# A second feed-forward input layer in seven half-width products instead of eight, with its weight sums split between GpSimd and VectorE

## The reference, cut to what matters

```
h  = x @ w_in                       # 1024 -> 2 x 2816 features
h  = conv_w[0]*h[t-1] + conv_w[1]*h[t] + conv_w[2]*h[t+1] + conv_b      # per feature, along the tokens
a, b = first 2816 features of h, last 2816 features of h
y  = (a * silu(b)) @ w_out          # 2816 -> 1024
```

## Time and profile before

| what | value |
|---|---|
| median of 3 runs | 1866.51 us (1865.86 to 1866.53) |
| time of the profiled execution | 1865.64 us, its span 1863.5 us |
| TensorE busy | 1715.4 us, 92% of the span |
| VectorE, ScalarE, GpSimd busy | 959.3, 377.4, 0.2 us |
| the changed stage, TensorE's first product to its last | 914.15 to 1066.17 us |
| granted TensorE clock there | 1.00 of full speed |

### The profile page before, as it was taken

How to read it: one execution, slowest core, us unless ns; L and a number is a source line. 1 busy time by engine, 2 the same in 40 slices (tenths; PEclk the granted TensorE clock), 3 DMA queues, 4 the chain that set the end, 5 groups by cost and what they waited for, 6 DMA issues and landing times.

```text
span 1863.5 us, 33795 instructions
## 1 busy us (share of the span) xinstructions
PE 1715.4 (92%) x14324; PEld 1358.6 (73%) x14324; DVE 959.3 (51%) x2032; ACT 377.4 (20%) x909; POOL 0.2 (0%) x4
## 2 busy tenths in 40 slices
PE   7999999999999999999999999999999767666676
PEld 4565687888888886776888898888887555545554
DVE  1488879666667328787544484577433111111112
ACT  0343413211110014222211102113402000000001
POOL 0000000000000000000000000000000000000000
PEclk9999999999999999999999999999999988888888
DMA  9524342222231214554343633331297999999997
GB/s 386 210 114 155 131 168 91 86 74 74 82 146 34 113 46 176 220 178 175 106 166 135 248 137 136 136 136 69 103 382 313 426 428 429 429 428 428 428 429 310
DMA packets 36164, 394.24 MB, mean 212 GB/s; under 512 B 3936, under 2 KB 7264, under 8 KB 14816
## 3 DMA queue, kind: packets, MB, share of 16 engines
q1 hardware_dynamic: 36064, 392.79, 52.3%
HBM read 391.72 MB, written 1.05 MB: 211 GB/s over the span
## 4 chain that ended last, share of the span: by engine, by line
PE 77%; DMA 19%; DVE 3%; issue 1%; ACT 0%; SPq 0%; DVEq 0%
PE bank L664 20%; DMA ring<-w_moe 19%; PE bank L1966 14%; PE bank L1680 11%; PE bank L2225 3%; PE bank L3788 3%; PE bank L2271 3%; PE bank L963 2%; PE bank L3554 2%; PE bank L2221 1%; PE bank L1268 1%; PE bank L718 1%; PE bank L872 1%; PE bank L2878 1%; PE bank L1253 1%; PE bank L2968 1%
## 5 line engine op out<-in xcount | busy, mean ns | idle before, releaser
L664 PE MATMUL bank<-layer_input,ring 128*128 128x256 f32 x1136 | 249.6, 380 | 0.0
L664 PEld LDWEIGHTS bank<-layer_input,ring 128*128 128x128 f32 x1136 | 214.4, 190 | 31.2 <-issue 2.7
L1680 PE MATMUL bank<-arena,ring 128*128 128x256 f32 (+1 forms) x940 | 167.4, 336 | 0.0
L1680 PEld LDWEIGHTS bank<-arena,ring 128*128 128x128 f32 x940 | 148.1, 191 | 14.6 <-issue 0.4
L3788 PE MATMUL bank<-arena 128*32 128x128 f32 x2008 | 77.8, 318 | 52.6 <-DMA arena<-w_moe 50.0
L3940 DVE TENSOR_TENSOR arena<-arena,bank 128x128 f32<-128x128 f32 x32 | 9.2, 288 | 218.1 <-PE bank L3788 218.1
L1966 PE MATMUL bank<-arena 128*128 128x256 f32 x504 | 115.7, 379 | 0.0
L3788 PEld LDWEIGHTS bank<-arena 128*32 128x32 f32 x2008 | 66.8, 128 | 64.4 <-DMA arena<-w_moe 60.1
L1966 PEld LDWEIGHTS bank<-arena 128*128 128x128 f32 x504 | 95.7, 190 | 13.2 <-DVE arena L2095 0.2
L3788 PE MATMUL bank<-ring,arena 128*32 128x128 f32 x1920 | 67.7, 301 | 27.6 <-DMA ring<-w_moe 27.3
L664 PE MATMUL bank<-arena 128*128 128x128 f32 (+2 forms) x400 | 86.6, 371 | 1.0 <-DVE arena L3768 1.0
(11 more groups left out here) (530 smaller groups left out, 2788.2 us busy)
## 6 DMA issues: line engine op xcount, KB each, us to landing
arena<-w_moe SPq DMA_DIRECT2D x45, 2048.0 KB, 25.8
ring<-w_moe SPq DMA_DIRECT2D x45, 2048.0 KB, 26.5
ring<-w_ffn_in SPq DMA_DIRECT2D x22, 2048.0 KB, 7.9
ring<-w_proj SPq DMA_DIRECT2D x7, 3072.0 KB, 10.3
ring<-w_ada_late SPq DMA_DIRECT2D x8, 2560.0 KB, 9.3
ring<-w_ffn_out SPq DMA_DIRECT2D x6, 2816.0 KB, 9.8
ring<-w_na_pair SPq DMA_DIRECT2D x5, 2048.0 KB, 7.9
arena<-w_far SPq DMA_DIRECT2D x16, 512.0 KB, 5.1
```

Source lines behind the costliest of these rows:

```text
L664: last = pe.matmul(out, a, b, start=(k == 0), stop=(k == len(lhs) - 1))
L1680: last = eng.matmul(out, w[:, k * P:(k + 1) * P], x[:, k, :], start=(start and k == 0), stop=(stop and k == half - 1), skip_group_check=True)
```

## The change

The second feed-forward input is rewritten. Weights and inputs are cut in two along k (features 0 to 511 and 512 to 1023) and in two along the tokens (128 and 128), and the value and gate rows give the other cut of the weights. Then for each f from 2 to 21 TensorE does seven products of 4 steps with 128 columns, in place of 16 steps with 256 columns. f = 0 and 1 (chunk 0) are done as before.

- Four sums of token blocks (128x512 each) are formed once, on VectorE.
- Four sums of weight blocks (128x1024) are needed for every pair of f. For pair 1 VectorE does all four. For pairs 2 to 10 GpSimd does the first and third and VectorE the second and fourth.
- ScalarE copies five running sums (128x128) per f out of PSUM, does the middle tap with the bias (from SBUF for f from 2 on), and the Silu as before.
- VectorE does three additions of 128x128 per f, the two shifted taps, and the value times gate.
- TensorE's first product of f waits for the taps of f - 2, and its third, fifth and seventh product each wait for a copy by ScalarE of what an earlier product left in the bank.
- The two ring places become three places of 4096 columns for this layer; chunk 0 has a load of its own, and chunks 1 and 2 are both issued when the attention's output product has ended.
- The loops become straight code. The stage behind it uses banks 0, 1 and 7 first (before, 5, 6 and 7), and its second product may start when the taps of f = 20 are done (before, f = 21). Two groups of semaphores are merged into one, and the stream's chunk numbers after this layer shift by one.

The core of the diff:

```diff
+OPEN_ROWS = (48, 32, 48, 32)
+PAIRS_IN, PAIR_PLACES = FT // 2, (0, 8192, 4096)
-          ("ffn_in1", 11, 4096), ("ffn_out1", 3, 5632),
+          ("ffn_in1", PAIRS_IN - 1, 4096), ("ffn_out1", 3, 5632),
...
+    def pool_program(self, pool):
+        summed, sums = self.sem("pool_summed"), self.pair_sums()
+        for c in range(2, PAIRS_IN):
+            (w11, w12), (w21, w22) = [[w.rearrange("p (f t) -> p f t", t=LAT) for w in row] for row in self.pair_weights(c)]
+            self.pair_loaded(pool, c)
+            pool.wait_ge(self.sem("ffn1_up_done"), 2 * SEVEN * (c - 1))
+            pool.tensor_tensor(sums[c % 2][0], w21, w22, ALU.add).then_inc(summed, 1)
+            pool.wait_ge(summed, 2 * (c - 2) + 1)
+            pool.tensor_tensor(w21, w11, w21, ALU.subtract).then_inc(summed, 1)
...
+    def load_pairs_in(self, sp):
+        sp.wait_ge(self.sem("y_ready"), RESIDUAL_BASE["na_o"] + 4)
+        sp.dma_start(self.pair_in(0), self.W["ffn_in1_a"][0]).then_inc(self.sem("second_in"), 16)
+        sp.wait_ge(self.sem("y_ready"), RESIDUAL_BASE["na_o"] + KT)
+        for c in range(1, PAIRS_IN):
+            g = FIRST["ffn_in1"] + c - 1
+            if c >= 3:
+                sp.wait_ge(self.sem("ffn1_up_done"), 2 * SEVEN * (c - 2))
+            sp.wait_ge(self.w_loaded[g % 2], 16 * (g // 2))
+            sp.dma_start(self.pair_in(c), self.W["ffn_in1"][c - 1]).then_inc(self.w_loaded[g % 2], 16)
...
+        def products(f):                                        # TensorE
+            a, b, d = self.pair_banks(e)
+            snap = 5 * (f - 2)
+            pe.wait_ge(s["up_used"], f - 1)
+            product(a, w11, A[0][0], True).then_inc(done, 1)
+            pe.wait_ge(s["sums_ready"], self.SUMS_FIRST + 2 * c + 1)
+            if c >= 2:
+                pe.wait_ge(self.sem("pool_summed"), 2 * (c - 1))
+            product(d, s1, t1, True).then_inc(done, 1)
+            pe.wait_ge(s["snapped"], snap + 1)
+            product(a, s2, t2, False).then_inc(done, 1)
+            product(b, w12, A[1][0], True).then_inc(done, 1)
+            pe.wait_ge(s["snapped"], snap + 3)
+            product(a, w21, t3, False).then_inc(done, 1)
+            product(d, s4, A[1][1], False).then_inc(done, 1)
+            pe.wait_ge(s["snapped"], snap + 4)
+            product(a, w22, t4, False).then_inc(done, 1)
...
+        for f in range(2, FT):                                  # VectorE
+            c = f // 2 + 1
+            if f % 2 and c < PAIRS_IN:
+                second_sum(c)
+            taps(f - 1)
+            if f == 2:
+                mult(0)
+            if f % 2 and c < PAIRS_IN:
+                fourth_sum(c)
+            add_left(f)
+            mult(f - 1)
+            add_right(f)
+            add_last(f)
...
+        for f in range(2, FT):                                  # ScalarE
+            a, b, d = self.pair_banks(f % 2)
+            for step, dst, src in ((1, v["snap"][f % 2][0], a), (2, v["snap"][f % 2][1], d), (3, v["snap"][f % 2][2], a)):
+                act.wait_ge(s["up_done"], f * SEVEN + step)
+                act.copy(dst, src).then_inc(snapped, 1)
+            silu(f - 1)
+            for step, dst in ((5, raw[1][:, P:LAT]), (7, raw[1][:, 0:P])):
+                act.wait_ge(s["up_done"], f * SEVEN + step)
+                act.copy(dst, a).then_inc(snapped, 1)
+            tap(f)
+        silu(FT - 1)
...
-                    eng.wait_ge(s["up_used"], used_0 + c - 1 - (o["turn"] if c == 0 else 0))
+                    eng.wait_ge(s["up_used"], used_0 + c - 1 - (c == 1 and o["ahead"]))
```

More of the change, by code:

```diff
@@ new lines, in ffn_pairs_act, with tap, silu @@
+    def ffn_pairs_act(self, act, s, v):
+        snapped, raw = s["snapped"], v["c"]
+        cw, cb = VOFF["conv_w"][0] + 3 * 2 * FT + 2 * FT, VOFF["conv_b"][0] + 2 * FT
+        def tap(f):
+            src = self.pair_sources(f, v)
+            if f < 2:
+                act.wait_ge(s["up_done"], SEVEN * (f + 1))
+                act.wait_ge(s["sums_ready"], 1)
+            else:
+                act.wait_ge(s["link"], 2 * f - 1)
+                act.wait_ge(s["hid_done"], f - 1)
+                act.wait_ge(snapped, 5 * (f - 1))
+            for x in (1, 0):
+                col = f + x * FT
+                last = act.activation(v["u"][f % 2][x], src[x], ACT.Identity, bias=self.V[:, cb + col:cb + col + 1],
+                                      scale=self.V[:, cw + col:cw + col + 1])
+            last.then_inc(s["tapped"], 1)
+        def silu(f):
+            act.wait_ge(s["up_used"], f + 1)
+            if f >= 2:
+                act.wait_ge(s["hid_done"], f - 1)
+            act.activation(v["sg"][f % 2], v["u"][f % 2][1], ACT.Silu).then_inc(s["gate_out"], 1)
+        tap(0)
+        tap(1)
+        silu(0)
+        for f in range(2, FT):
[9 more added lines that the diff above has]
+        silu(FT - 1)
@@ L1623, in split_layer @@
         places = [spare[0][:, 0:256], spare[0][:, 256:512], spare[1][:, 0:256], spare[1][:, 256:512], self.N[:, 7680:7936]]
-        self.split_out(who, eng, s, o | dict(gain=g, bias=b, width=T, layer=0, segs=(0, 1), token_sums=sums, spare=places,
+        self.split_out(who, eng, s, o | dict(ahead=False, gain=g, bias=b, width=T, layer=0, segs=(0, 1), token_sums=sums, spare=places,
                                              chunk=lambda c: c // o["per"], turn=0, write_input=write_input))
@@ L2821, in mixer @@
         self.split_out(who, eng, ffn, dict(
-            name="ffn_out1", source=self.hidden[:, :, 0:LAT], half=HALF_LAST, nk=FT, steps=LAST_STEPS, sums=2 * FT, used=FT,
-            per=1, gate=5, layer=1, segs=(1, 1), width=LAT, sum_at=0, last=7, turn=1, gain=g, bias=b,
+            name="ffn_out1", source=self.hidden[:, :, 0:LAT], half=HALF_LAST, nk=FT, steps=LAST_STEPS, sums=2 * FT - 2, used=FT, ahead=True,
+            per=1, gate=5, layer=1, segs=(1, 1), width=LAT, sum_at=0, last=7, turn=0, gain=g, bias=b,
             chunk=LAST_IN_RING.index, far=self.last_far(), squares=[self.A[:, k, CTX:T] for k in range(KT)],
-            between=lambda part: self.fill(eng, (2, 1, 6)[part], self.bank[1]),
+            between=lambda part: self.fill(eng, (2, 1, 6)[part], self.bank[0]),
             token_sums=[holes[:, near, 0:P], holes[:, far, 0:P], holes[:, near, P:LAT]],
```

255 lines of the change are left out of this document (159 added, 96 removed).

## The result

The change made the kernel slower by 7.5 us. Its median over 6 runs is 1874.05 us (1872.09 to 1875.46), against 1866.52 us (1865.83 to 1867.62) for the kernel before in 6 runs beside it. The ratio is 1.004, with a 95% interval of 1.0029 to 1.0052. I had forecast 1859.9 us. The time lies inside my range, but on the other side of zero from my likeliest case.

The account below looks back on a forecast made before the run. TensorE's instructions were taken to bound the changed stage. 13.0 saved - 2.7 opening - 3.1 handoff - 0.6 end = 6.6 us, with GpSimd's contention at nothing: median 1866.51 to 1859.9, whole range 1857 to 1883.

Parts of the forecast that it names:

- TensorE's work: Changed stage, f = 2 to 21: seven half-width products save 0.65 us per f, 13.0 us in all.
- The opening: Before f = 2: TensorE's first product waits 2.7 us for VectorE's taps, which follow eight sums.
- The handoff: Third product of each turn: waits for ScalarE's copy behind its taps, 0.16 us a turn, 3.1 us for 19.
- The end: After TensorE's last product: VectorE's sums of the next stage start 0.6 us later, lost in full.
- The sum without contention: Whole kernel: if GpSimd does not delay VectorE, 6.6 us saved, median 1859.9; chance 0.41.
- GpSimd's sums: Two sums of 128x1024 per pair: 2.4 us each, twice VectorE's row, bounds 1.22 and 8.8.
- ScalarE's tables: Rival, every turn: tap and Silu alternate, so the table loads twice; 25 us, 1885; chance 0.04.
- the small waits of odd turns: Rival, VectorE's odd turns: the saving is lost in small waits; chance 0.05.
- GpSimd as the bound: Rival, each pair: sums of 8.8 us outlast a pair's 12.8 us; 44 us lost, about 1904; chance 0.03.
- What they do to VectorE: While GpSimd and VectorE both read SBUF: cost between nothing and complete exclusion, counted as nothing.
- my first rival: Both GpSimd sums exclude VectorE's taps: 2T - 2.5 a pair, T a sum's time; 22.8 us, 1882.7; chance 0.27.
- the second rival: Exclusion, second sum after all four taps: third product of odd f 1.05 us late; 10.4 in all, 1870.3; chance 0.20.

## Why the prediction was wrong

**TensorE's work: right.** 0.65 us per f was saved. Turns without GpSimd take 6.44 us (half of 12.88), which is the 6.26 of the products and 0.18 of handoff.

**The opening: right in cause, 0.4 us too high.** TensorE went on 2.32 us late, not 2.7, released by VectorE's taps. The whole stage began 0.46 us later than before (914.61 for 914.15), VectorE and TensorE alike. Counted from its start, VectorE let TensorE go after 16.21 us, where I had reckoned 16.55 (930.7 less 914.15): its eight sums took 7.45 us from the last residual write (921.47 to 928.92) and not 7.6, and the four taps 1.79 and not 1.89.

**The handoff: right**, 0.18 us a turn against 0.16. Moving the copy gave 0.19 back. It doesn't show as idle time, as I had said it would: the third product starts 0.98 us behind the second in place of 0.89 (974.37 behind 973.39) and takes 1.16 us in place of 1.06. With the copy moved both are gone.

**The end: right**, 0.44 us against 0.6.

**The sum without contention: right.** 7.1 us less in the stage with GpSimd's sums taken off (152.02 to 144.95), against 13.0 - 2.7 - 3.1 = 7.2, and 1859.22 us against 1859.9. ScalarE's tables, the small waits of odd turns and GpSimd as the bound all played no part: the stage has one table load where it had eleven before, pairs without GpSimd take 12.88 us, and GpSimd's busy time is 4.77 us of a pair's 14.45.

**GpSimd's sums: size right, 2.35 to 2.42 us against 2.4.** The Trainium skill ("GPSIMD Engine Reference", section 3.1) had led to an estimate of 2.25 us, half of what it states for 2048 columns. The trace lies 0.1 to 0.2 us above it.

**What they do to VectorE: this is the step that failed.** It stood in the prediction as "they speak for nothing, so the sum goes by nothing". I named as the nearest rows TensorE and VectorE reading the same buffers, and let them stand for GpSimd and VectorE. They do not even show that: in this stretch TensorE reads the inputs and the ring, VectorE PSUM and the arena. So the term was put at nothing without a row for it. It measured 12.6 us. The runs showed that a VectorE instruction with both tensors in SBUF stands still while a GpSimd instruction reads SBUF, with one input or two. It doesn't when GpSimd only writes, nor when VectorE's other tensor is in PSUM. The Trainium skill states this contention and both exceptions ("SBUF — State Buffer", section "Who interferes with whom"). Every trace here agrees: taps of 0.48 us grew to 2.57 beside two-input sums and to 1.01 beside copies, and kept 0.48 beside fills and with a tensor in PSUM. That it is a standstill and not a slower pace is seen from the ends: four delayed instructions of different kinds and starts (a tap beside a sum, a tap beside a copy, and two products beside sums) each end 0.28 to 0.29 us behind the recorded end of what GpSimd did. A clash over one buffer doesn't explain it, since GpSimd's second sum touches the ring alone and VectorE's taps the arena and the vectors.

**The mechanism is my first rival's, at little more than half its price** (12.6 us for 22.8). As it says, the first sum takes its turn while VectorE is idle, one tap slips in, and the second sum goes ahead of the other three. The taps of the turn shown above, one by one:

```profile
974.20 1.25 DVE L1669 SCALAR_TENSOR_TENSOR arena<-arena,vectors 128x255 f32<-128x255 f32 x1 [2.11 <-ACT arena L1737]
975.37 2.57 DVE L1669 SCALAR_TENSOR_TENSOR arena<-arena,vectors 128x255 f32<-128x255 f32 x1
977.97 0.88 DVE L1669 SCALAR_TENSOR_TENSOR arena<-arena,vectors 128x255 f32<-128x255 f32 x2
```

Its formula gave 2T - 2.5 = 2.3 us a pair; TensorE's seventh product was late by 1.46 (wanted at 978.05, started at 979.51). The difference lies in two places. The taps ended 6.36 us after the turn's start (at 978.85, from 972.49) and not 7.0. Some 0.4 us of that is that the first and the second tap end only 0.28 us behind the recorded end of the sum they waited for, though a tap takes 0.48. And Silu, copy and wake-up took 0.66 us, not 0.85. Another 0.1 us a pair goes in the seventh product itself, which takes 1.16 us behind its wait in place of 1.06. In the opening, for which I had added 4.4 us more, the exclusion cost nothing, because the first taps read PSUM and nobody waited for the one product that was held up: the rival's condition was two SBUF inputs, and I had not held it against those taps, whose form stands in the code.

So the eight pairs lost 12.6 us in place of nothing. Against the 7.1 gained in the stage, with the 0.44 of the end and 0.46 by which the stage began later, the handover comes 6.3 us later, and 7.5 was measured. That 0.46 is scatter: the stage starts between 913.53 and 915.52 in the ten experiments. The rest lies behind the handover and stays open.

**Smaller slips.** Half of the second rival's 0.20 and the 0.05 of the last make 0.15 for a time within 0.2%, not 0.14. And chunk 1 is called early though by my own bound it lands at 924.3, after the 923.7 at which it is wanted; the sum that needs it began at 924.04, right behind the one before, so it cost nothing.

**Left open.** Why the granted clock dipped for 3 us behind the same wait of 2.16 us in four profiles and not in five others isn't settled: one profile of each kernel doesn't tell chance from cause. Open too is what VectorE's instruction does to GpSimd's when it comes first: the second sum takes 2.42 us in the pairs and 2.35 in the opening, and no run tells why.

## What to carry to other kernels

Work on GpSimd isn't free because GpSimd is idle: before moving a read from SBUF there, look which VectorE instructions with two SBUF inputs fall in its time, and who waits for them. Where VectorE has room, as here (busy 10.46 of 12.88 us with all four sums), it does the same sum in half the time and without the exclusion; otherwise give GpSimd short pieces, places where VectorE reads PSUM, or work that only writes. And a wait taken away is worth its length only up to what is late next: 2.16 us gone here gave 0.7.

## What the runs showed of the hardware

- The stall of VectorE stands in the duration of its instruction (0.48 us up to 2.57), not in the idle time before it, and it ends with the GpSimd instruction. A table of waits alone shows ScalarE waiting for VectorE, and VectorE never for GpSimd.
- A GpSimd instruction that waits gets in between two VectorE instructions that follow each other without a gap: the second sum began at 975.24, while the first of four taps was still recorded.
- GpSimd's durations over 128 partitions in float32: sum of 1024 columns 2.36 us, of 512 columns 1.33, copy of 1024 1.04, fill of 1024 0.95. VectorE's sum of 1024 is 1.22.
- TensorE, after standing still for 2.16 us, ran at a granted clock of 1.00 in some profiles and near 0.5 for about 3 us in others. The dip made the stage 1.6 us longer.
